# Differential attention scores of an encoder kernel on one Trainium2 core: contraction over 64 rows for each map instead of 128 rows with zeros

## The reference

```python
def diff_attention(q1, q2, k1, k2, v, lam):
    ...
        bias = -slopes[:, None, None] * jnp.abs(qpos[:, None] - kpos[None, :])[None]
        p1 = jax.nn.softmax(jnp.einsum('bqhd,bkhd->bhqk', q1b, k1).astype(jnp.float32) * scale + bias, axis=-1)
        p2 = jax.nn.softmax(jnp.einsum('bqhd,bkhd->bhqk', q2b, k2).astype(jnp.float32) * scale + bias, axis=-1)
        p = (p1 - lam * p2).astype(v.dtype)
        return jnp.einsum('bhqk,bkhd->bqhd', p, v)
```

## Time and profile before

| | |
|---|---|
| median of 3 runs | 880.38 us (880.32 to 880.66) |
| the profiled execution, its own time | 880.17 us |
| its span | 878.4 us |
| TensorE busy | 744.7 us (85%) |
| TensorE weight loads | 629.8 us (72%) |
| VectorE busy | 592.4 us (67%) |
| ScalarE busy | 517.8 us (59%) |
| GpSimd busy | 229.7 us (26%) |

### The profile page before, as it was taken

How to read it: one execution, slowest core, us unless ns; L and a number is a source line. 1 busy time by engine, 2 the same in 40 slices (tenths; PEclk the granted TensorE clock), 3 DMA queues, 4 the chain that set the end, 5 groups by cost and what they waited for, 6 DMA issues and landing times. The chain is left out here.

```text
span 878.4 us, 13714 instructions
## 1 busy us (share of the span) xinstructions
PE 744.7 (85%) x4057; PEld 629.8 (72%) x4057; DVE 592.4 (67%) x999; ACT 517.8 (59%) x960; POOL 229.7 (26%) x291
## 2 busy tenths in 40 slices
PE   3999999978887898978999289999999999999800
PEld 3998899956775676757888267888777777777600
DVE  6831210468895778771376869898888888888425
ACT  2252321588885788871114437888877888777312
POOL 5110000135453443422022014223222222331126
PEclk9999999999997999979999579999999999999965
DMA  8213110000001100006623639999999999999453
GB/s 301 75 49 96 48 60 1 1 21 1 1 0 41 57 1 1 1 0 212 270 120 145 233 126 340 368 390 387 388 367 384 387 389 389 387 380 371 160 168 143
DMA packets 70985, 159.50 MB, mean 182 GB/s; under 512 B 7456, under 2 KB 15648, under 8 KB 70944
## 3 DMA queue, kind: packets, MB, share of 16 engines
q1 hardware_dynamic: 66048, 141.16, 42.4%
q0 software_dynamic: 4896, 17.83, 7.9%
HBM read 139.57 MB, written 19.40 MB: 181 GB/s over the span
## 5 line engine op out<-in xcount | busy, mean ns | idle before, releaser
L1943 DVE TENSOR_TENSOR eDl<-rawD,eDh 128x1024 fp32r<-128x1024 f32 x68 | 80.2, 1220 | 13.9 <-ACT eDh L1887 13.8
L1943 DVE TENSOR_TENSOR eUl<-rawU,eUh 128x1024 fp32r<-128x1024 f32 x68 | 79.7, 1222 | 7.1 <-ACT eUh L1887 4.2
L1943 DVE TENSOR_TENSOR eGl<-rawG,eGh 128x1024 fp32r<-128x1024 f32 x64 | 76.2, 1223 | 9.0 <-ACT eGh L1887 7.9
L2015 POOL DMA_INDIRECT acc_rows<-yg,idx_s x17 | 31.3, 1842 | 152.7 <-ACT yg L1912 152.7
L1887 ACT ACTIVATE eGh<-rawG 128x1024 fp32r<-128x1024 f32 x64 | 66.1, 1057 | 5.9 <-DMA rawG<-in_w_gate 4.6
L1835 PE MATMUL bank<-eGh,xgT_h 128*128 128x512 f32 x136 | 57.2, 421 | 14.2 <-DVE xgT_l L1948 13.0
L1887 ACT ACTIVATE eUh<-rawU 128x1024 fp32r<-128x1024 f32 x64 | 63.5, 1053 | 7.2 <-DMA rawU<-in_w_up 7.2
L1887 ACT ACTIVATE eDh<-rawD 128x1024 fp32r<-128x1024 f32 x64 | 64.0, 1055 | 0.0
L480 DVE TENSOR_TENSOR w_l<-w_raw,w_h 128x1024 fp32r<-128x1024 f32 (+2 forms) x16 | 17.7, 1147 | 66.3 <-ACT w_h L379 66.3
L312 PE MATMUL bank<-w_h,xT_h 128*128 128x256 f32 (+1 forms) x192 | 55.5, 289 | 2.7 <-DVE xT_l L472 2.7
L1856 PE MATMUL bank<-eDh,hT_h 128*128 128x512 f32 x136 | 53.7, 395 | 2.2 <-DVE hT_l L1960 2.2
(11 more groups left out here) (317 smaller groups left out, 2292.3 us busy)
## 6 DMA issues: line engine op xcount, KB each, us to landing
rawG<-in_w_gate SPq DMA_DIRECT2D x68, 512.0 KB, 14.2
rawU<-in_w_up SPq DMA_DIRECT2D x68, 512.0 KB
rawD<-in_w_down SPq DMA_DIRECT2D x68, 512.0 KB, 11.0
w_raw<-in_w_in SPq DMA_DIRECT2D x7, 1024.0 KB, 5.3
wo_raw<-in_w_o SPq DMA_DIRECT2D x16, 256.0 KB, 5.3
acc_rows<-ax SPq DMA_DIRECT2D x7, 512.0 KB, 2.6
x_rows<-res SPq DMA_DIRECT2D x6, 512.0 KB, 2.8
res<-acc_rows SPq DMA_DIRECT2D x6, 512.0 KB, 5.7
```

The lines of the kernel that those rows point to most:

```text
L1943: nc.vector.tensor_tensor(wl_[X][i][:], raw_of(X, t, i)[:], f32(wh_[X][i][:]), ALU.subtract).then_inc(s_lo[X], 1)
L2015: pool.indirect_dma_start(out=acc_rows, out_offset=bass.IndirectOffsetOnAxis(ap=idx_s[:, 0:1], axis=0), in_=yg[:], in_offset=None, bounds_ ...
```

## The change

The query has one high and one low copy per sequence, of 128 partitions, made by one ScalarE copy and one VectorE subtraction. The scores of map m take rows 64m to 64m + 63 of the query copy and of the key copy, so each matmul contracts over 64 rows. The order alternates between the maps: high x high for map 0 and 1, low x high for both, high x low for both. The wait for the two banks (s_bias) stands once, ahead of both maps, and asks for both maps of tile i-2. The cleared rows and their semaphore go, on GpSimd, and on TensorE as a wait. The semaphore counts follow. The arithmetic is otherwise the same.

```diff
-    q_h = [[at(f"q_h{x}{m}", 78 + 6 * m + 4 * x, [P, SEQS[x][1]], FR) for m in range(2)] for x in range(2)]
-    q_l = [[at(f"q_l{x}{m}", 80 + 6 * m + 3 * x, [P, SEQS[x][1]], FR) for m in range(2)] for x in range(2)]
+    q_h = [at(f"q_h{x}", 78 + 4 * x, [P, SEQS[x][1]], FR) for x in range(2)]
+    q_l = [at(f"q_l{x}", 80 + 3 * x, [P, SEQS[x][1]], FR) for x in range(2)]
...
-                    wait(pe, s_zero, 2 * x + 2)
-                    wait(pe, s_ql, 4 * h + 2 * x + 2)
+                    wait(pe, s_ql, 2 * h + x + 1)
                     wait(pe, s_kl, 2 * h + x + 1)
+                qs = slice(qt * P, (qt + 1) * P)
+                wait(pe, s_bias, 2 * g - 2)
+                out = [psum[2 * (i % 2) + m][:, 0:n] for m in range(2)]
+                half = [slice(DHD * m, DHD * m + DHD) for m in range(2)]
                 for m in range(2):
-
-                    wait(pe, s_bias, 2 * g - 4 + m + 1)
-                    qs = slice(qt * P, (qt + 1) * P)
-                    out = psum[2 * (i % 2) + m][:, 0:n]
-                    nc.tensor.matmul(out, q_h[x][m][:, qs], kk_h[x][:], start=True, stop=False)
-                    nc.tensor.matmul(out, q_l[x][m][:, qs], kk_h[x][:], start=False, stop=False)
-                    nc.tensor.matmul(out, q_h[x][m][:, qs], kk_l[x][:], start=False, stop=True).then_inc(s_sc, 1)
+                    nc.tensor.matmul(out[m], q_h[x][half[m], qs], kk_h[x][half[m], :], start=True, stop=False)
+                for m in range(2):
+                    nc.tensor.matmul(out[m], q_l[x][half[m], qs], kk_h[x][half[m], :], start=False, stop=False)
+                for m in range(2):
+                    nc.tensor.matmul(out[m], q_h[x][half[m], qs], kk_l[x][half[m], :], start=False, stop=True).then_inc(s_sc, 1)
...
                 nc.scalar.activation(kk_h[x][:], dkT[:, h, t0:t0 + n], ACT.Copy).then_inc(s_qkh, 1)
-                for m in range(2):
-                    r = slice(64 * m, 64 * m + 64)
-                    nc.scalar.activation(q_h[x][m][r, :], dqT[r, h, t0:t0 + n], ACT.Copy).then_inc(s_qkh, 1)
+                nc.scalar.activation(q_h[x][:], dqT[:, h, t0:t0 + n], ACT.Copy).then_inc(s_qkh, 1)
...
-            for x in range(2):
-                for m in range(2):
-                    r = slice(64 - 64 * m, 128 - 64 * m)
-                    nc.gpsimd.memset(f32(q_h[x][m][r, :]), 0.0)
-                    nc.gpsimd.memset(f32(q_l[x][m][r, :]), 0.0).then_inc(s_zero, 1)
...
-            pool.wait_ge(s_zero, 4)
...
-                for m in range(2):
-                    r = slice(64 * m, 64 * m + 64)
-                    wait(dve, s_qkh, 6 * h + 3 * x + m + 2)
-                    nc.vector.tensor_tensor(q_l[x][m][r, :], dqT[r, h, t0:t0 + n], f32(q_h[x][m][r, :]), ALU.subtract).then_inc(s_ql, 1)
+                wait(dve, s_qkh, 4 * h + 2 * x + 2)
+                nc.vector.tensor_tensor(q_l[x][:], dqT[:, h, t0:t0 + n], f32(q_h[x][:]), ALU.subtract).then_inc(s_ql, 1)
```

More of the change, by code:

```diff
@@ L585, in encoder_trunk @@
     s_alibi = sem("alibi_landed")
-    s_zero = sem("zero_rows_ready")
     s_qkh, s_ql, s_kl = sem("diff_qk_high"), sem("diff_q_low"), sem("diff_k_low")
@@ L906, in cut_q @@
                 t0, n, _ = SEQS[x]
-                for m in range(2):
-                    r = slice(64 * m, 64 * m + 64)
-                    wait(dve, s_qkh, 6 * h + 3 * x + m + 2)
-                    nc.vector.tensor_tensor(q_l[x][m][r, :], dqT[r, h, t0:t0 + n], f32(q_h[x][m][r, :]), ALU.subtract).then_inc(s_ql, 1)
+                wait(dve, s_qkh, 4 * h + 2 * x + 2)
+                nc.vector.tensor_tensor(q_l[x][:], dqT[:, h, t0:t0 + n], f32(q_h[x][:]), ALU.subtract).then_inc(s_ql, 1)
             def cut_k(h, x):
                 t0, n, _ = SEQS[x]
-                wait(dve, s_qkh, 6 * h + 3 * x + 1)
+                wait(dve, s_qkh, 4 * h + 2 * x + 1)
                 nc.vector.tensor_tensor(kk_l[x][:], dkT[:, h, t0:t0 + n], f32(kk_h[x][:]), ALU.subtract).then_inc(s_kl, 1)
```

## The result

The changed kernel takes 896.8 us (median of 4 runs, 895.18 to 900.73) against 880.5 us before: a ratio of 1.019, 95% interval 1.016 to 1.023. It is 16 us slower where 8 us less was forecast.

What follows compares the result with a forecast made beforehand. VectorE in its own order, then ScalarE, was taken to bound the differential stage, not the matmuls. Gains 1.3 (start) + 5.0 (VectorE) + 2.4 (ScalarE waits) = 8.7, less 1.0, net 7.7 us, gave 872.7 us, range 868 to 878.

Steps and rivals of the forecast that it cites:

- The single copies: Query cuts on VectorE: one instruction of each pair goes, q_l from 11.3 to 4.3 us, gaining 5.0 at head changes.
- new waits: Between VectorE and ScalarE, nearly equally busy and each in order: 1.0 us of the gain given back.
- the start: Start of the differential stage: first biased tile begins at 185.5 instead of 186.82, gain 1.3 us, 0.7 without overlap.
- waits for dpT_h: VectorE waiting for ScalarE, mainly at head changes and query cuts: 2.4 us less, between 1.3 and 4.3.
- rival B: ScalarE takes over at 18.4 us per head, only its own savings come through: 876 us, chance 0.12.
- The overlap: Half-height score matmuls on different rows running together: 0 to 3.5 us per head of TensorE time, taken as likelier.
- rival A: Half-height score matmuls don't overlap, or drain eats the overlap; 3.0 us of gain lost: 875.7 us, chance 0.18.
- The changes of height: TensorE, two per tile around the scores: 0.16 to 0.39 us each if the array empties, 1.9 to 4.7 per head.
- TensorE has slack: Differential stage's middle heads: TensorE's starts fill 16.5 of 22.7 us per head, leaving 6 us.
- rival C: TensorE idles more between bursts, the differential stage's clock stays low, 26.0 us per head: 891 us, chance 0.05.
- The condition that C gave: For rival C to decide, the low clock must hold for more than 0.75 of the differential stage.
- Rival D: Half-height score matmuls stream slower, at twice the time 23.5 us per head on TensorE: 882 us, chance 0.03.

Runs made afterwards that it cites:

- the warm start: The changed kernel plus six full-height matmuls at the differential stage's start, while TensorE waits for the first query cuts: 896.0 us, one run of four at 874.6.

## Why the prediction was wrong, step by step

The single copies. VectorE's q_l, beside the earlier trace rows, and its first biased tile, beside the earlier trace rows:

```profile
L899 DVE TENSOR_TENSOR q_l<-dqT,q_h 128x512 fp32r<-128x512 f32 x4 | 2.9, 718 | 0.0
L899 DVE TENSOR_TENSOR q_l<-dqT,q_h 128x256 fp32r<-128x256 f32 x4 | 1.7, 416 | 0.0
...
185.94 0.69 DVE L926 CUSTOM_DVE_ANT_0 ee<-bank,bias_t 128x512 f32<-128x512 f32 x1 [0.23 <-DVE bias_t L918]
```

4.6 us in place of 11.3 (4.3 was forecast), and the first tile begins 3.90 us behind the table's issue where it was 5.21: 1.3 us, as forecast. With every matmul at full height the stage gains 8.5 us; the sum had 8.7, or 7.7 with 1.0 given back for new waits. That the total agrees is in part luck, for its parts don't. In that kernel, without overlap and at the low clock, the first biased tile starts at 186.84, 5.01 us behind the table's issue, so the start gives 0.2 and not 1.3. VectorE's waits for dpT_h fell from 7.7 to 4.8 us, 2.9 where 2.4 was forecast. New waits did come: its waits for scores rose from 0.7 to 2.6 us and those for the table's scaling from 0.5 to 1.0. Against that the two middle heads together are 6.5 us shorter (45.40 to 38.93) where 20.7 us a head made 4.0, and the clock is 1.00 in them where it was 0.94; how much of the gain is the clock's no run tells. ScalarE did not take over (rival B): heads of 19.1 and 19.9 us are below the 20.7 foreseen.

The overlap (rival A's question) is there, shown by the pairs 0.24 us apart. The changes of height cost about 0.32 us per tile at the low clock; the bounds, 0.16 to 0.39 each for two, or 0.32 to 0.78 per tile, were read at the full clock, and it lies at their lower end.

The step that failed is the one on TensorE. "TensorE has slack", 16.5 of 22.7 us per head, was read at the full clock and carried into the changed stage, and the sum has no term for this stage's clock. The runs showed a clock of 0.54 in place of 0.92, a head in which TensorE needs 27.2 us, and VectorE waiting 17.3 us for scores. Of this the prediction had the effect and its price, as rival C, with 0.05 of the chance: it put the head at 26.0 us at the lower level and the kernel at 891. Measured are 27.1 and 896.8. The difference is in two terms. The extra around the scores, changes of height above all, was left out of that head, 2.6 us, and the halving was made of rounded spacings (0.23 doubled is 0.46, where the low clock has 0.42). And three and a half heads was short: from the last head's scaling to the stage's end it was 34.1 us (247.26 to 281.31) and is 45.5 (254.21 to 299.67), +11.4; the two middle heads give +8.8; up to the second head's scaling -2.3. Sum +17.9, and the span grew by 17.8, so all of it lies in this stage.

What misled me was the evidence set against C. A stretch in which TensorE was busy 0.36 of 2 us with the clock at 1.00 seemed to say that this stage could lose a lot of activity. Read on, the same trace weakens that: the clock is 0.59 from 245 us, two stretches later. C's reason, idle time between bursts, fits how the clock fell in the changed kernel (behind 0.60, 1.11 and 1.19 of 2 us) but not why it stayed down: from 195 to 293 us TensorE is busy all the time, at 0.50. The three full-height matmuls per tile leave TensorE idle time as well and lose only stretches, and the two maps on the same rows have none from 192 us on and lose everything. So in these traces TensorE's busy time alone doesn't tell the clock. The condition that C gave, three quarters of the stage at the low level, was met: a mean of 0.54 is about nine tenths of it.

Rival D, half height streaming slower in itself, is refuted by the spacing of 0.24 us at the full clock.

What stays open: in what way the height counts, why the changed kernel's clock stayed at 0.50 in the 14 us of full-height work behind its last pair while it came back there in the run with the maps in turn, and why the same program sometimes keeps the clock (874.6 in one run of four of the warm start, not profiled). The runs show the two ends and a middle, not a rule.

## What to carry to other kernels

Matmuls on half of the array's rows do run in pairs, in both orders of issue that were tried, but a stage that relies on them can lose TensorE's clock for nearly all of its length, and then pays on every other matmul in it. Before halving the height of matmuls, ask whether TensorE sets the pace at half the clock, not at the full one, and read the granted clock of the stage first when the result disagrees. Here the savings on the other engines needed the half height, since one query copy serves both maps, so the full height had to be added beside it: of the kernels that compute the whole reference the fastest has full-height matmuls whose results are thrown away, at 0.9925 of the kernel before.

## What the runs showed of the hardware

- Score matmuls of 64 rows start in pairs, 0.24 us apart for 512 columns at the full clock and 0.42 at the low one, and they do so even where the program issues all of one map before the other.
- Changing between 64 and 128 rows costs about 0.32 us for a change there and back, at the low clock: 0.34, 0.60 and 0.56 us into, within and out of the half-height scores, against 0.21, 0.54 and 0.43 in a kernel without changes.
- With TensorE busy 54.18 of 54.18 us the granted clock was 0.50 where six of each tile's matmuls had half height; with the same matmuls at full height it was 1.00 in the two middle heads.
- The clock fell behind stretches in which TensorE was busy 0.60, 1.11 and 1.19 of 2 us, and then stayed at 0.50 from 195 us to the stage's end with TensorE busy 2.00 of 2 us; the last 14 us of that were full-height work alone.
- Adding two full-height matmuls per tile, whose results are thrown away, shortened the stage from 117.6 to 102.9 us, and with six more at its start and two more per tile in the first head and the next one's first tile to 92.5.
